# A hybrid decoder layer on one core: conditioning in pieces by contraction rows, u and its first use by token parts

## The chip, the cores and the metric

The kernel runs on one core of a Trainium2 chip. The metric is device time in microseconds. TensorE (PE) multiplies, VectorE (DVE), ScalarE (ACT) and GpSimd (POOL) do the elementwise work, and SyncE (SP) issues most of the DMAs. Data comes from HBM into SBUF (128 partitions); TensorE writes into eight banks of PSUM.

## The reference, cut to what matters

One layer is computed for a prompt of 1024 tokens and for 8 samples of one token each, with the same weights. Both have conditioning vectors c (one for the prompt, eight for the samples), so `mod` has nine rows of 6144.

```python
x = layernorm(x, ln_in_g, ln_in_b)
mod = silu(c) @ w_ada + b_ada                     # 9 x 6144
sh1, sc1, g1, sh2, sc2, g2 = split(mod, 6)
u = x * (1 + sc1) + sh1
proj = u @ w_in          # s_b, s_c, s_h, z, xbc, dt, gates
...                      # short convolution, SSD scan, merged by gates
x = layernorm(ALPHA * x + (1 + g1) * (merged @ w_o), ln_mix_g, ln_mix_b)
u2 = x * (1 + sc2) + sh2
x = layernorm(ALPHA * x + (1 + g2) * moe(u2), ln_ffn_g, ln_ffn_b)
```

Only the first third of `mod` (sh1 and sc1, 2048 columns) is needed to make u; g1 and sh2 (the second third) and sc2 and g2 (the last) are used after the scan. w_ada has 1024 contraction rows and 6144 columns, 25 MB in float32.

## The kernel before

Each engine has one program, written out by hand; the engines wait for each other on semaphores. 1032 tokens (1024 and 8) stand as nine tiles of 128, the last with 8 rows. Contraction over 1024 goes in eight steps of 128 rows (`k`).

**Start.** SP loads c, the x tiles (`load_x`, four buffers) and w_ada in 12 groups of 512 columns, 2 MB each, into three buffers (`load_wada`). DVE's `norm(i)` makes the input layernorm of a tile: statistics, the root on ACT (`std`), then two wide operations (L1223, L1226) with mean, ln_in_g, reciprocal root and ln_in_b. POOL stores the normed tile to `x0_dram` for the residual. On TensorE `mod_group(q)` (L1858) makes 512 columns of `mod` with c as the stationary operand, 9 columns wide, so all results lie in PSUM partitions 0 to 8. DVE adds the bias (`add_mod`, L1231). After four groups TensorE turns the 16 blocks of shift and scale into columns (L1876) and small weight rows too (L1882, L1889). Then `turn_x(i)` (L1868) turns a tile of x, and ACT makes u from it with `scale` and `bias` per partition (`ut`, L903), between the other eight groups. When all is there, TensorE makes the 32 dt columns of all tiles (L1903), ACT and DVE split u into `u_hi` and `u_lo` (L918, L1290), for projections in three parts of a float.

**Turns.** `turn(g)` makes six units of 128 projection columns (x, x, B, C, z, z of a head group), each in three token parts of 344 columns (`SUB`): 18 steps, counted from 0, in the order `STEPS`, a projection of 24 matmuls each (L1912 to L1914). The weights of a unit are split on ACT (`high`, L923) and POOL (`low`, L760), three slots deep. Turn 0 has projections alone, with the sums of dt*A in between (L2009 to L2012) and the spread of the samples' rows (L2015), and DVE's convolutions of its units at its end. Turns 1 to 8 run the SSD scan of the group before beside the projections.

**w_o stage.** Late in the kernel, for each tile, TensorE makes merged @ w_o (L2128), and DVE multiplies by 1 + g1, adds ALPHA times the stored x (L1599), norms and makes u2 (L1596 to L1620).

## Time and profile before

| | us |
|---|---|
| median of 3 runs (2714.0 to 2715.81) | 2715.81 |
| the profiled execution, its own time | 2713.93 |
| its span, first to last instruction | 2711.8 |
| TensorE busy | 2438.1 |
| DVE busy | 1616.0 |
| ACT busy | 1174.5 |
| POOL busy | 544.0 |
| mean granted TensorE clock, share of full | 0.956 |

The busy time of an engine tells little by itself; a stage is read by who waits for whom in it. The time that the whole takes beside the span (2.1 us) lies around the first and the last instruction. Times in the rows below are from the start of the span.

### The profile page before, as it was taken

The numbers are of one execution on the slowest core, as the hardware profiler recorded it, in microseconds if no ns is written. First come the engines' busy times: TensorE is split into PE (matmuls) and PEld (weight loads), VectorE is DVE, ScalarE is ACT, GpSimd is POOL, SyncE is SP. The second block draws the span as 40 slices with busy tenths as digits, with TensorE's granted clock in tenths as the row PEclk, the third lists the DMA queues.
The fourth block names the chain that finished last, engine by engine and source line by source line (L and its number), as shares of the span: only waits on it lengthen the run. The fifth ranks groups of instructions, "written<-read, shape, count | busy, mean of one in ns | idle before, by whom it ended". The sixth has DMA issues, their size and how long they took to land. (4 is left out here: it accounts for less than half of the span.)

```text
span 2711.8 us, 32410 instructions
## 1 busy us (share of the span) xinstructions
PE 2438.1 (90%) x13028; PEld 1994.9 (74%) x13028; DVE 1616.0 (60%) x2502; ACT 1174.5 (43%) x1480; POOL 544.0 (20%) x309
## 2 busy tenths in 40 slices
PE   6889999999999999999999999999579999999960
PEld 2289888888889889666999988855257777777740
DVE  3336988988988983000133321145758888888869
ACT  0334677667677675000000000000147777777751
POOL 0011221221121120000344411100013223232320
PEclk8979999999999999999999999999789999999985
DMA  7722233233233224212111131121369999999963
GB/s 262 271 67 80 62 96 101 59 95 97 63 90 103 63 82 152 67 39 54 39 47 47 47 102 41 30 89 58 121 213 348 340 350 353 354 347 337 339 218 141
DMA packets 255525, 397.56 MB, mean 147 GB/s; under 512 B 17571, under 2 KB 167723, under 8 KB 255321
## 3 DMA queue, kind: packets, MB, share of 16 engines
q1 hardware_dynamic: 232368, 344.63, 38.6%
q0 software_dynamic: 14080, 34.61, 3.3%
q10 hardware_dynamic: 8928, 16.26, 1.9%
q8 instruction: 103, 1.69, 0.3%
q14 instruction: 46, 0.38, 0.0%
HBM read 364.66 MB, written 48.22 MB: 152 GB/s over the span
## 5 line engine op out<-in xcount | busy, mean ns | idle before, releaser
L1912 PE MATMUL bank<-u_hi,w_pairs 128*128 128x344 f32 x1344 | 446.6, 332 | 9.1 <-DVE u_lo L1290 9.1
L1913 PE MATMUL bank<-u_lo,w_pairs 128*128 128x344 f32 x1344 | 431.2, 321 | 0.0
L1914 PE MATMUL bank<-u_hi,w_pairs 128*128 128x344 f32 x1344 | 431.1, 321 | 0.0
L1651 DVE TENSOR_TENSOR we_parts<-u_whole,we_parts 128x2048 fp32r<-128x2048 f32 x129 | 295.1, 2287 | 60.0 <-ACT we_parts L1131 59.7
L1131 ACT ACTIVATE we_parts<-u_whole 128x2048 fp32r<-128x2048 f32 x129 | 247.1, 1917 | 51.5 <-PE bank L2176 26.3
L1912 PEld LDWEIGHTS bank<-u_hi,w_pairs 128*128 128x128 f32 x1344 | 255.2, 190 | 14.0 <-DVE u_lo L1290 9.3
L760 POOL TENSOR_TENSOR w_pairs<-arena,w_pairs 128x1024 fp32r<-128x1024 f32 x56 | 150.7, 2692 | 545.1 <-ACT w_pairs L923 544.9
L1913 PEld LDWEIGHTS bank<-u_lo,w_pairs 128*128 128x128 f32 x1344 | 254.7, 190 | 3.9 <-issue 3.8
L1914 PEld LDWEIGHTS bank<-u_hi,w_pairs 128*128 128x128 f32 x1344 | 254.5, 189 | 0.0
L2034 PE MATMUL bank<-arena 128*128 128x344 f32 x768 | 222.2, 452 | 0.0
L2174 PE MATMUL bank<-we_parts,x_parts 128*128 128x512 f32 x512 | 209.8, 410 | 3.3 <-DVE we_parts L1651 1.9
L2034 PEld LDWEIGHTS bank<-arena 128*128 128x128 f32 x768 | 145.9, 190 | 76.0
L2176 PE MATMUL bank<-we_parts,x_parts 128*128 128x512 f32 x512 | 201.2, 393 | 0.0
L2175 PE MATMUL bank<-we_parts,x_parts 128*128 128x512 f32 x512 | 200.4, 391 | 0.0
L1374 DVE SCALAR_TENSOR_TENSOR arena<-arena 128x512 f32<-128x512 f32 (+3 forms) x192 | 158.9, 827 | 3.4
L1912 PE MATMUL bank<-u_hi,w_even 128*128 128x344 f32 x480 | 155.8, 325 | 2.3 <-DVE arena L1562 1.7
L1651 DVE TENSOR_TENSOR we_parts<-arena,we_parts 128x2048 fp32r<-128x2048 f32 x64 | 146.6, 2291 | 12.0 <-ACT we_parts L1131 12.0
L1913 PE MATMUL bank<-u_lo,w_even 128*128 128x344 f32 x480 | 153.3, 319 | 0.0
L1914 PE MATMUL bank<-u_hi,w_even 128*128 128x344 f32 x480 | 153.3, 319 | 0.0
L1535 DVE TENSOR_TENSOR arena<-arena,bank 128x344 f32<-128x344 f32 x24 | 12.3, 513 | 229.7 <-PE bank L2034 229.7
L1081 ACT ACTIVATE arena<-bank 128x344 f32<-128x344 f32 x24 | 11.0, 458 | 293.2 <-PE bank L1914 293.2
L1003 ACT ACTIVATE arena<-bank 128x344 f32<-128x344 f32 x168 | 74.5, 448 | 138.2 <-PE bank L1914 136.8
(340 smaller groups left out, 5029.5 us busy)
## 6 DMA issues: line engine op xcount, KB each, us to landing
u_whole<-in_w_moe_dram SPq DMA_DIRECT2D x128, 1024.0 KB, 7.4
arena<-in_w_moe_dram SPq DMA_DIRECT2D x64, 1024.0 KB, 7.5
arena<-in_w_in_dram SPq DMA_DIRECT2D x88, 512.0 KB, 5.4
arena<-in_w_ada_dram SPq DMA_DIRECT2D x12, 2048.0 KB, 11.6
arena<-cum_dram ACTq DMA_DIRECT2D x62, 256.0 KB, 3.1
yb_dram<-arena POOLq DMA_DIRECT2D x8, 1032.0 KB, 5.0
arena<-in_state_ssm_dram SPq DMA_DIRECT2D x16, 512.0 KB, 5.6
out_dram<-arena SPq DMA_DIRECT2D x16, 512.0 KB, 4.5
```

What stands on the lines that cost most here:

```text
L760: pool.tensor_tensor(pair_lo[u % 3], wslot[u], pair_hi[u % 3].bitcast(F32), ALU.subtract).then_inc(unit_split, 1)
L1003: act.activation(dst[:, part * SUB:(part + 1) * SUB], banks[s % 3][:, 0:SUB], ACT.Copy).then_inc(raw_ready, 1)
L1131: act.activation(w_his[parts_of(n, j)], wraw[slot], ACT.Copy).then_inc(whi_ready, 1)
L1374: last = dve.scalar_tensor_tensor(dst[:, start:hi], src[:, start - back:hi - back], w(3 - back), dst[:, start:hi], ALU.mult, ALU.add)
L1651: dve.tensor_tensor(w_los[v], wraw[slot], w_his[v].bitcast(F32), ALU.subtract).then_inc(wlo_ready, 1)
L1912: pe.matmul(out, hi[:, k, :], u_hi[:, k, at], start=(k == 0), stop=False)
L1913: pe.matmul(out, hi[:, k, :], u_lo[:, k, at], start=False, stop=False)
L1914: last = pe.matmul(out, lo[:, k, :], u_hi[:, k, at], start=False, stop=(k == KD - 1))
L2034: last = pe.matmul(banks[first + part][:, 0:SUB], wslot[slot][:, k, :], yb[1 - half][:, k, part * SUB:(part + 1) * SUB], start=(half == 0 ...
L2174: pe.matmul(out, xt_hi[b][:, at], w_his[v][:, cols], start=(kk == 0), stop=False)
L2175: pe.matmul(out, xt_hi[b][:, at], w_los[v][:, cols], start=False, stop=False)
L2176: last = pe.matmul(out, xt_lo[b][:, at], w_his[v][:, cols], start=False, stop=(kk == KD - 1))
```

## The change

**Conditioning.** w_ada is loaded in 24 pieces by contraction rows: 128 rows and one third of the columns (2048), 1 MB, with 8 KB in a row. `mod_piece(q)` makes four matmuls of 512 columns per piece; each writes its own 32 partitions of one PSUM bank (`acc[32 * j:32 * j + 32]`), and the stationary c is padded with zeros to 32 columns. A third has eight pieces. The first third is made at the start, the others within the second half of turn 0, one or two pieces behind a projection. The bias is broadcast to 32 partitions four times per third, and DVE adds it in one operation per third. SP stores the last two thirds to `mod_dram` (POOL did it once before).

**u.** ln_in_g and ln_in_b are turned into columns and put into scale and shift; `norm(i)` has one wide operation. Nine x buffers instead of four. ACT (`u_left`) and DVE (`u_right`) make half a tile of u each; `u_high`, `u_low` and `dt_rows` go tile by tile. `x0_dram` then holds x without ln_in_g and ln_in_b; they are applied on DVE in the w_o stage (`residual`), with two more loads of broadcast rows.

**Turn 0.** The first nine steps go by token parts (`STEPS0`); a part starts when the three tiles of u that it needs are split. Tiles 5 to 8 are turned between the first four steps, and dt of tiles 3 to 8 between the first five. ACT makes dt's exponentials behind its ninth copy. DVE adds the second third's bias ahead of the convolutions and the last third's behind them.

```diff
-            r0 = Room(Y0, W0)
-            wada = [r0.take(KD * 512).rearrange("p (k c) -> p k c", k=KD) for _ in range(3)]
-            xr = [r0.take(D) for _ in range(4)]
...
+        xr = [arena[:, XR0 + i * D:XR0 + (i + 1) * D] for i in range(TILES + 1)]
+        wada = [arena[:, 2 * D * x:2 * D * (x + 1)] for x in range(7)] + [arena[:, YST0:YST0 + 2 * D]]
+        late = (YST0, HS0, HS0 + 2 * D)
+        wada += [arena[:, late[x % 3]:late[x % 3] + 2 * D] for x in range(2 * KD)]
...
+        STEPS0 = [(u, part) for part in range(3) for u in range(3)] + STEPS[9:]
...
             def load_wada(q):
-                if q >= 3:
-                    sp.wait_ge(mod_done, q - 2)
-                sp.dma_start(wada[q % 3], w_ada_v[:, :, q * 512:(q + 1) * 512]).then_inc(wada_landed[q % 3], 16)
+                third, k = q // KD, q % KD
+                if q >= 4:
+                    sp.wait_ge(mod_done, q - (2 if q >= 11 else 3))
+                sp.dma_start(wada[q], w_ada_v[:, k, 2 * D * third:2 * D * third + 2 * D]).then_inc(wada_landed[q % 4], 16)
...
+            turn(0, False, range(3))
+            sp.wait_ge(dt_raw, 9)
+            sp.wait_ge(x0_stored, 9 * 16)
+            for third in range(1, 3):
+                load_bada(third)
+            for q in range(8, 11):
+                load_wada(q)
+            turn(0, False, range(3, 6))
+            for q in range(11, 16):
+                load_wada(q)
             sp.wait_ge(cols_copied, 5)
...
+            for q in range(18, 24):
+                load_wada(q)
+            for third in range(1, 3):
+                sp.wait_ge(mod_added, third + 1)
...
-                st.did(dve.scalar_tensor_tensor(x, x, mv[0:rows, i % 4, 0:1], ln_g[0:rows, :], ALU.subtract,
-                                                ALU.mult))
                 st.settle()
-                dve.scalar_tensor_tensor(x, x, mv[0:rows, i % 4, 3:4], ln_b[0:rows, :], ALU.mult,
-                                         ALU.add).then_inc(x0_ready, 1)
+                dve.tensor_scalar(x, x, mv[0:rows, i, 0:1], mv[0:rows, i, 3:4], ALU.subtract,
+                                  ALU.mult).then_inc(x0_ready, 1)
...
+            u_right(0)
+            for i in range(1, TILES + 1):
+                u_right(i)
+                u_low(i - 1)
+            u_low(TILES)
...
+            residual(0)
             for i in range(TILES + 1):
...
                 dve.tensor_tensor(u, u, sh2, ALU.add).then_inc(u2_ready, 1)
+                if i < TILES:
+                    residual(i + 1)
...
+            def mod_piece(q):
+                third, k = q // KD, q % KD
+                pe.wait_ge(wada_landed[q % 4], 16 * (q // 4 + 1))
+                if k == 0 and third:
+                    pe.wait_ge(mod_added, third)
+                acc = banks[(0, 3, 4)[third]]
+                for j in range(4):
+                    last = pe.matmul(acc[32 * j:32 * j + 32, :], c_t[:, k, :], wada[q][:, 512 * j:512 * j + 512],
                                      start=(k == 0), stop=(k == KD - 1))
                 last.then_inc(mod_done, 1)
...
+            for i in range(5, TILES + 1):
+                turn(0, (i - 5,))
+                turn_x(i)
+                if i == 5:
+                    dt_rows(3)
+                dt_rows(i - 1)
+            turn(0, (4,))
+            dt_rows(TILES)
+            turn(0, range(5, 10))
+            mod_piece(8)
+            for s in range(10, 18):
+                turn(0, (s,))
+                if s == 11:
+                    pe.wait_ge(dta_ready, 1)
...
+                if s == 13:
+                    pe.wait_ge(spread_ready, 1)
+                    pe.matmul(bank7, ones[0:NS, :], spread, start=True, stop=True).then_inc(spread_done, 1)
+                    mod_piece(15)
+                else:
+                    q = 2 * s - 11 - (s > 13)
+                    for x in range(2):
+                        mod_piece(q + x)
```

TensorE, the start, before: the c rows are turned (L1848), then groups of the conditioning (`9x512`), small rows (L1876 to L1889), and x turns between further groups.

```order
L1848 MATMUL bank<-arena 128x9 x8
L1858 MATMUL bank<-arena 9x512 x32
L1876 MATMUL bank<-arena 128x9 x16
L1882 MATMUL bank<-arena 128x21 x8
L1889 MATMUL bank<-arena 128x29 x32
L1868 MATMUL bank<-arena 128x128 x8
L1858 MATMUL bank<-arena 9x512 x8
```

And now: L1946 is a matmul of a piece (`32x512`), L1957 a turn of x, L1981 the turn of scale and shift, L1990 dt of a tile. The last two rows come twice more before the first projection.

```order
L1934 MATMUL bank<-arena 128x9 x8
L1946 MATMUL bank<-arena 32x512 x16
L1966 MATMUL bank<-arena 128x23 x8
L1971 MATMUL bank<-arena 128x29 x32
L1957 MATMUL bank<-arena 128x128 x16
L1946 MATMUL bank<-arena 32x512 x16
L1981 MATMUL bank<-arena 128x128 x4
L1957 MATMUL bank<-arena 128x128 x8
L1990 MATMUL bank<-arena,u_whole 128x32 x8
```

Before, all 96 conditioning matmuls and all 72 of dt stood ahead of the first projection; now 32 of the conditioning and 24 of dt do, and the rest is among the projections.

TensorE in turn 0, behind projection 11, in the kernel now: L2004 is the end of that projection, L2113 to L2115 the sums of dt*A, L1946 two pieces, L2002 the next projection.

```order
L2004 MATMUL bank<-u_hi,w_pairs 128x344
L2113 MATMUL bank<-arena 128x128 x2
L2114 MATMUL bank<-arena 128x256
L2115 MATMUL bank<-arena 128x256
L1946 MATMUL bank<-arena 32x512 x8
L2002 MATMUL bank<-u_hi,w_pairs 128x344
```

The sums stood behind projection 5 before, with no pieces around them.

SP's queue of DMAs from the first units' weights to turn 1, before (in brackets the semaphores that an issue waits for):

```order
L497 DMA arena<-in_w_in_dram 128x8x128 [waits mod_added]
L497 DMA arena<-in_w_in_dram 128x8x128 x5
L497 DMA arena<-in_w_in_dram 128x8x128 [waits unit_split] x2
L561 DMA cum_dram<-arena 128x2x128 [waits cols_copied]
L567 DMA arena<-cum_dram 128x512 [waits cum_stored,dt_ready]
L567 DMA arena<-cum_dram 128x512
L520 DMA arena<-in_state_ssm_dram 128x8x128 x2
L497 DMA arena<-in_w_in_dram 128x8x128 [waits unit_split] x4
```

And now:

```order
L487 DMA arena<-in_w_in_dram 128x8x128 [waits unit_split] x3
L483 DMA arena<-in_b_ada_dram 32x512 [waits x0_stored,dt_raw]
L483 DMA arena<-in_b_ada_dram 32x512 x7
L478 DMA arena<-in_w_ada_dram 128x2048 [waits mod_done] x3
L487 DMA arena<-in_w_in_dram 128x8x128 [waits unit_split] x3
L478 DMA arena<-in_w_ada_dram 128x2048 [waits mod_done] x5
L584 DMA cum_dram<-arena 128x2x128 [waits cols_copied]
L478 DMA arena<-in_w_ada_dram 128x2048 [waits mod_done] x2
L591 DMA arena<-cum_dram 128x512 [waits cum_stored,dt_ready]
L591 DMA arena<-cum_dram 128x512
L478 DMA arena<-in_w_ada_dram 128x2048 [waits mod_done] x6
L600 DMA mod_dram<-arena 9x512 [waits mod_added]
```

The 16 loads of w_ada's last two thirds, which stood ahead of the first units, are now spread among turn 0's other issues, each with a wait for a piece made.

## Rows read from the trace of the kernel before

**Rows 1.** The page's busy table: busy us (share of the span), instructions.

```profile
PE 2438.1 (90%) x13028; PEld 1994.9 (74%) x13028; DVE 1616.0 (60%) x2502; ACT 1174.5 (43%) x1480; POOL 544.0 (20%) x309
```

**Rows 2.** Busy time by stage: window, length, PE, PEld, DVE, ACT, POOL, PEclk, DMA, GB/s.

```profile
63.50:135.10 71.60, 64.75 (x193) 17.65 (x193) 27.15 (x55) 24.09 (x70) 3.19 (x6) 0.99 0.76 270
135.10:162.00 26.90, 26.80 (x144) 26.59 (x144) 0.19 (x1) 9.25 (x6) 4.68 (x2) 0.53 0.61 164
...
171.04:243.23 72.19, 72.19 (x443) 71.10 (x444) 33.09 (x57) 23.09 (x38) 14.51 (x6) 0.98 0.21 53
```

**Rows 3.** Order of time, 108 to 117 us: start, us, engine, line, count.

```profile
108.68 1.09 PE L1868 MATMUL bank<-arena 128*128 128x128 f32 x8
...
109.87 2.90 ACT L903 ACTIVATE u_whole<-bank,arena 128x128 f32<-128x128 f32 x8 [3.47 <-PE bank L1868]
...
109.92 7.04 PE L1858 MATMUL bank<-arena 128*9 128x512 f32 x16 [0.15 <-DMA arena<-in_w_ada_dram]
```

**Rows 4.** Order of time, the split of u and the first projection.

```profile
162.03 8.96 DVE L1290 TENSOR_TENSOR u_lo<-u_whole,u_hi 128x2064 fp32r<-128x2064 f32 x4 [26.74 <-PE bank L1903]
...
171.04 0.66 PE L1912 MATMUL bank<-u_hi,w_pairs 128*128 128x344 f32 x1 [9.12 <-DVE u_lo L1290]
```

**Rows 5.** Busy time by stage while the first loads run; DMA share and GB/s last.

```profile
4.00:12.00 8.00, 0.00 (x0) 0.00 (x0) 1.66 (x4) 1.73 (x3) 0.00 (x0) 1.00 1.03 398
12.00:20.00 8.00, 7.75 (x13) 1.44 (x14) 0.00 (x0) 0.00 (x0) 0.00 (x0) 1.00 1.06 195
...
24.00:48.00 24.00, 18.34 (x38) 3.68 (x39) 13.87 (x20) 0.59 (x2) 1.87 (x3) 0.79 1.04 396
```

**Rows 6.** Order of time on DVE: a norm of tile 5, and wide tensor_scalars later.

```profile
77.15 1.29 DVE L1216 BATCH_NORM_STATS2 arena<-arena 128x6 f32<-128x512 f32 x2 [4.65 <-DMA arena<-in_x_prompt_dram]
...
79.12 1.27 DVE L1223 SCALAR_TENSOR_TENSOR arena<-arena 128x1024 f32<-128x1024 f32 x1
...
1779.32 2.51 DVE L1586 TENSOR_SCALAR u_whole<-u_whole 128x1024 f32<-128x1024 f32 x4 [0.21 <-DMA arena<-in_b_route_e_dram]
```

**Rows 7.** Busy time by stage: two x turns, dt, and the first projection's start.

```profile
61.61:63.50 1.89, 1.89 (x9) 1.56 (x8) 0.83 (x4) 0.00 (x0) 0.00 (x0) 0.50 0.01 4
...
116.89:117.90 1.01, 1.01 (x9) 0.85 (x8) 0.68 (x1) 0.00 (x0) 0.00 (x0) 1.00 1.06 389
...
171.04:174.47 3.43, 3.43 (x12) 3.43 (x13) 1.09 (x5) 2.98 (x5) 0.00 (x0) 0.50 0.00 0
...
137.00:162.00 25.00, 24.93 (x129) 24.69 (x128) 0.00 (x0) 7.35 (x6) 4.68 (x2) 0.50 0.57 154
```

**Rows 8.** Order of time on PE in turn 1: matmuls that write 64 partitions each.

```profile
252.27 0.66 PE L1955 MATMUL bank<-arena 128*64 128x128 f32 x8
252.86 0.33 PE L1943 MATMUL bank<-arena 128*128 128x128 f32 x1
```

**Rows 9.** Order of time: the first and the last step of the dt chain.

```profile
171.44 0.45 ACT L932 ACTIVATE arena<-arena 128x288 f32<-128x288 f32 x1 [27.09 <-DVE arena L1296]
...
182.23 0.17 DVE L1329 TENSOR_TENSOR arena<-arena 8x32 f32<-8x32 f32 x1
```

**Rows 10.** Order of time: DVE's first operation of turn 1, in brackets its wait.

```profile
243.97 0.29 DVE L1386 TENSOR_TENSOR arena<-bank,arena 128x128 f32<-128x128 f32 x1 [9.77 <-PE bank L1946]
```

**Rows 11.** DMA issues: 1 MB loads from the page; landing of the w_ada loads.

```profile
u_whole<-in_w_moe_dram SPq DMA_DIRECT2D x128, 1024.0 KB, 7.4
...
DMA to landing us min/median/max: 8.6/11.6/21.2
```

**Rows 12.** The w_o stage: DVE's waits (us, times, longest), a wide operation, the last tile.

```profile
DVE arena L1596 <- PE bank L2128: 63.2, 9, 11.4
...
L1618 DVE TENSOR_TENSOR arena<-arena,u_whole 128x1024 f32<-128x1024 f32 (+1 forms) x9 | 11.0, 1223 | 0.3
...
1919.79 1.28 DVE L1596 TENSOR_TENSOR arena<-bank,u_whole 8x512 f32<-8x512 f32 x2 [7.10 <-PE bank L2128]
```

More of the change, by code:

```diff
@@ L1051, in _ @@
             act.activation(decay, cend, ACT.Exp).then_inc(wend_ready, 1)
-            turn(0, range(7, 18))
+            turn(0, range(12, 18))
             for g in range(1, GROUPS + 1):
@@ L1244, in _, with add_mod @@
+            def add_mod(third):
+                dve.wait_ge(mod_done, KD * third + KD)
+                if third:
+                    dve.wait_ge(small_landed, (16 + 8) * 16)
+                dve.tensor_tensor(mod[third], banks[(0, 3, 4)[third]][:, :], bada[third], ALU.add).then_inc(mod_added, 1)
+            for i in range(4):
+                norm(i)
+            dve.wait_ge(cols_turned, 1)
+            src = bank6[:, 0:KD * (ROWS_C + 2)].rearrange("p (k r) -> p k r", k=KD)
             for a, b in ((0, 3), (19, 21)):
@@ L1282, in _ @@
-            last.then_inc(ut_s_ready, 1)
+            for i in range(4, TILES + 1):
+                norm(i)
+            add_mod(0)
+            dve.wait_ge(cols_turned, 4)
+            dve.wait_ge(cols_copied, 3)
+            turned = banks[5][:, :].rearrange("p (c j m) -> p j c m", c=4, j=4)
+            by_col = dict(j=2)
+            scale4, shift4 = (x.rearrange("p (j c) m -> p j c m", j=2) for x in (scale_t, shift_t))
+            for j in range(2):
+                st.did(dve.tensor_scalar(scale4[:, j], turned[:, 2 + j, :, 0:MROWS], 1.0, None, ALU.add))
@@ L1895, in _ @@
-            turn_x(TILES)
-            pe.wait_ge(ut_ready, TILES)
-            pe.wait_ge(ut_s_ready, 1)
-            for i in range(TILES + 1):
-                rows = P if i < TILES else NS
-                for k in range(KD):
-                    last = pe.matmul(bank7[0:rows, i * HEADS:(i + 1) * HEADS], uT[:, k, i * P:i * P + rows],
-                                     w_dt[:, k, :], start=(k == 0), stop=(k == KD - 1))
-            last.then_inc(dt_raw, 1)
-            pe.wait_ge(u_lo_ready, KD // 2)
+            turn_x(0)
@@ new lines, in _, with dt_rows @@
+            pe.wait_ge(cols_copied, 1)
+            turn_x(1)
+            for q in range(4, 8):
+                mod_piece(q)
+            pe.wait_ge(mod_added, 1)
+            for cb in range(4):
+                last = pe.transpose(banks[5][:, cb * P:(cb + 1) * P], mod[0][:, cb * P:(cb + 1) * P], ident)
+            last.then_inc(cols_turned, 1)
+            def dt_rows(i):
+                rows = P if i < TILES else NS
+                pe.wait_ge(ut_ready, min(i + 1, TILES))
+                pe.wait_ge(ut_s_ready, i + 1)
+                for k in range(KD):
+                    last = pe.matmul(banks[5][0:rows, i * HEADS:(i + 1) * HEADS], uT[:, k, i * P:i * P + rows],
+                                     w_dt[:, k, :], start=(k == 0), stop=(k == KD - 1))
+                last.then_inc(dt_raw, 1)
@@ L1908, in projection @@
+            for i in range(2, 5):
+                turn_x(i)
+                dt_rows(i - 2)
             def projection(out, hi, lo, part):
@@ L1922, in sub @@
                 def sub(s):
-                    u, part = STEPS[s]
+                    u, part = step_of(g, s)
+                    if g == 0 and s in (0, 3, 6):
+                        pe.wait_ge(u_lo_ready, s + 3)
                     if part == 0:
```

337 lines of the change are left out of this document (177 added, 160 removed).

## The prediction

> **What bounds the kernel now.** I read the page's busy table first, then the busy time of each engine by stage, then the order of time at the start. TensorE is busy 90% of the span [rows 1], so the reader looks for the stretches where it works at something that need not be there, or sparsely. The stage table [rows 2] shows one: the first projection of turn 0 starts at 171.04 us. Until then TensorE makes the conditioning, turns x and makes the dt columns. Turn 0 itself then takes 72.19 us with TensorE never idle. So what counts is when turn 1 can begin: 243.23 us now. After it the two kernels run the same projections in the same order, up to the w_o stage, so a gain up to there reaches the end unless that stage gives it back.
>
> Three things lie ahead of 171 us. The conditioning: 12 groups of 16 matmul records, 7.04 us each at the full clock [rows 3], 84 us of TensorE altogether. The dt columns: 26.80 us [rows 2], nearly all at half the clock. And the split of u, which waits for all of them: DVE's 8.96 us with TensorE idle for 9.12 us [rows 4]. The loads are not idle either: 24 to 48 us moved 396 GB/s at a DMA share of 1.04 [rows 5], so the first 40-odd us are near what the DMAs give.
>
> **The change part by part.** I rebuild the time at which turn 1 starts.
>
> *To the scale and shift of u (before: at 55 us, but with the matmuls of the other two thirds following until 133).* Only the first third, 8 pieces of 1 MB, is needed. With x (4.2 MB), the pieces (8.4 MB) and some 0.9 MB of small rows, 13.5 MB must land. At 396 to 398 GB/s [rows 5] that is 34 us from the first issue at 1.5 us; the stretch from 12 to 20 us, where the small rows moved at only 195 GB/s, costs another 4 to 6: the last piece lands near 42. DVE is later than that. It now norms x tiles 4 to 8 before it adds the bias. A norm takes 1.97 us until the first of its two wide operations, which takes 1.27 [rows 6]; now one two-scalar operation stands there for both, which I put at 0.7 to 1.1 us, since a 1024-wide tensor_scalar is at 0.63 (four in 2.51, [rows 6]). So 2.8 us a norm. The five start when the small columns are turned. That stands behind piece 3 (some 26 us) and, at half the clock, 6 to 7 us of turns, so at 33; they end at 47. Bias 0.7, four turns 1.2, six small DVE operations 1.7: **51 us** (45 if the small rows hold up less, 58 if they hold up more). The dropped ln_g and ln_b rows save 1 MB of loads and one wide operation a tile; that is in these numbers.
>
> *Three token tiles before the first projection (before: all nine).* The first projection of a part of 344 columns needs u tiles 0 to 2. TensorE turns x (8 turns: 1.89 us at half the clock, 1.09 at full [rows 3, 7]) and makes that tile's dt (16 records; 129 records took 25 us at half the clock [rows 7], so 3.1 to 3.4). ACT and DVE make half a tile each: ACT's eight took 2.90 [rows 3], so four 1.45. The split of a tile is 1.05 on ACT and 1.2 on DVE and follows tile by tile. TensorE is the slowest: 3 x 5.4 at half the clock, plus 1.5 before and 1.2 behind, is **19 us**; at the full clock 3 x 2.85 + 2.7, so 11.5. I take the half clock, because in the two stretches with such work, 61.61 to 63.50 and 137 to 162, the granted clock was 0.50 [rows 7]. The first projection then starts at 70 us.
>
> *Turn 0 itself:* the same 18 projections in another order, **72 us**, with its first 3.43 us at half the clock [rows 7], as now.
>
> *Moved into turn 0:* turns of four tiles (3 x 1.09 + 0.7) and dt of six (5 x 1.8 + 0.9 at the full clock, twice that at half): **14 us**, up to 28 where the clock falls between projections.
>
> *Sixteen pieces in turn 0.* A piece is 4 matmuls of 512 columns, 8 records. One after another a record takes 0.427 us (7.04/16 with its gap, [rows 3]), so a piece 3.42. Each of the four writes its own 32 PSUM partitions. The nearest row is the one where matmuls write 64 partitions each in turn: 8 records of 128 columns took 0.59 us until the next matmul started [rows 8], while 8 turns of 128 columns on the whole array took 1.01 until the next, from 116.89 to 117.90 [rows 7]. Records of the first start in pairs: four pairs of 0.107 are 0.43, and the rest, 0.16, is the way in and out. So groups run side by side. For four groups I take 2 x 0.427 plus 0.14, **1.0 us a piece, 16 us**. The ends are 0.87 (nothing for the way in) and 1.72 (only two of four side by side).
>
> The Trainium skill, page "TensorE: Matmul & The Clock Gate", section "Measured speedup vs the span model", has 2.38 times for three column tiles, not 3. By that a piece would be an estimated 1.08 us and the term 17 instead of 16. Its row shows less overlap than ours of two groups; no row here shows three or four.
>
> *Loads of these pieces.* They go through three places, a load being issued once the piece three before is made. The 15 pieces from step 10 on have a cover of 8 x 3.8 + 15 x 1.0 = 45 us; with a landing time L they take at least 5 x (L + 1.0). A 1 MB load of this size landed in a median of 7.4 us under a full load of DMAs [rows 11], which gives 42. It just fits; I put **3 us** for single waits (0 to 10).
>
> *Waits added in turn 0.* ACT makes dt's exponentials only behind its copy of projection 8. The chain takes 10.8 us (171.44 to 182.23, [rows 9]), so it is done 12.5 us after projection 8; TensorE asks for it behind three projections and three pieces, 14 us later: hidden by these 1.7 us. Queued behind it on ACT are copies 9 to 11, which TensorE needs three projections on. DVE's bias add of the second third stands ahead of all convolutions; after it DVE has 20 us of them, against 4 projections and 8 pieces, 23 us. They end together with turn 0, where DVE now waits 9.77 us [rows 10]: that cover is nearly used up, and if it is gone turn 1 starts a microsecond or two late. On SP, loads of state, the sums and the third's stores are behind waits for pieces; the state is asked for 30 us into turn 1. Nothing else waits there.
>
> *Two more DVE operations a tile in the w_o stage* (ln_g and ln_b put onto the stored x): 9 x 2 x 1.22 us [rows 12], 22 us of DVE. DVE waits for TensorE 63.2 us over the nine tiles there, 7.1 before the last [rows 12], and TensorE doesn't wait for it. 2.45 fits into each wait: **0**, and 22 if that cover were gone.
>
> *Sum:* 51 + 19 + 72 + 14 + 16 + 3 = **175 us** for the start of turn 1, against 243.2: 68 us less. The profiled execution took 2713.9 us (span 2711.8); 68 off is 2646. The median of the runs shown is 1.9 higher, so **2647 us**.
>
> **The rivals.** (1) *The four column groups run one after another*, so the change doesn't do what its form asks. Then 16 x 2.4 = 39 us come back in turn 0, and some 8 in the start, where pieces 4 to 7 stand behind the turns: 2694. For it speaks that no row has four groups or streams this long; against it the pairs. (2) *Turn 0 is paced by loads.* The 2 MB conditioning loads landed in a median of 11.6 us [rows 11]. With that as L, 5 x 12.6 = 63 against 45: 18 us back, 2665. For it: they go out behind other waits on one queue. Against: half the size, long rows. (3) *The start runs at the full clock*: 7.5 us less there and 1.7 less in the first projection, 2638. (4) *Slower than before*: the same mechanism as (2) with loads that land late enough. It decides from L = 22 us on, since 5 x 23 - 45 is 70, and 2716 or more comes out. The latest load of the conditioning took 21.2 us [rows 11], but it was twice as large and stood behind the small rows.
>
> **How the numbers follow.** Forecast 0.66, (1) 0.09, (2) 0.12, (3) 0.10, (4) 0.02, and 0.01 for a time within 0.2% of before. 0.2% is 5.4 us, about what a measurement of this kernel tells from no change. The likeliest stays: 2647. For the range, the lows (45, 11.5, pieces at 0.87, no waits) would give 2623 if all came together, the highs (58, moved work at half the clock, pieces at 1.72, 10 us of waits) 2686. Not all meet: I take 2628 to 2676. That holds the forecast, (2) and (3) and leaves out (1) and (4). Faster: 0.66 + 0.09 + 0.12 + 0.10 = 0.97; same 0.01; slower 0.02.
>
> **What would show it.** In the changed kernel's rows: the first u_hi projection near 70 us and the first scores of turn 1 near 175; the scale written near 51; the granted clock between 50 and 70 us (0.50 here, 1.00 for (3)); a piece's 8 records starting in fours within about a microsecond, not 0.43 apart; TensorE idle before a piece for its load not above 1 us (more is (2)); DVE still idle before its w_o additions. I am wrong most easily in the start, where the DMAs, DVE's five norms and the clock each can move it by 5 to 8 us.

## The result and the profile after

| | before | changed kernel | forecast |
|---|---|---|---|
| median of four runs, us | 2715.81 | 2648.2 | 2647 |
| lowest and highest run | 2714.0, 2715.93 | 2646.19, 2651.25 | range 2628 to 2676 |
| profiled execution, its own time | 2713.93 | 2651.25 | |
| its span | 2711.8 | 2649.5 | |
| first projection of turn 0 starts (in the span) | 171.04 | 74.78 | 70 |
| first scores of turn 1 start | 243.23 | 180.27 | 175 |

The ratio of the changed kernel to the one before is 0.9754, with a 95% interval of 0.9742 to 0.9766: 67 us less. The profiled execution is the slowest of the four runs. In it turn 1 begins 63.0 us earlier, and the span is 62.3 us shorter, so 0.7 us were given back behind turn 0. The engines' busy line, answering to [rows 1]:

```profile
PE 2383.2 (90%) x13016; PEld 1987.3 (75%) x13016; DVE 1628.0 (61%) x2532; ACT 1164.9 (44%) x1453; POOL 543.3 (21%) x309
```

TensorE is busy 55 us less in all. Busy time by stage (window, length, PE, PEld, DVE, ACT, POOL, PEclk, DMA, GB/s), answering to [rows 2, 5]: the start at half the clock; turn 0 as a whole, then its part with the moved work and its part with the pieces.

```profile
47.80:78.52 30.72, 22.00 (x97) 19.77 (x98) 17.11 (x36) 15.41 (x29) 9.88 (x5) 0.50 0.61 187
74.78:180.27 105.49, 105.16 (x699) 89.70 (x699) 43.95 (x84) 32.99 (x57) 14.15 (x6) 0.95 0.54 193
74.78:111.56 36.78, 36.78 (x249) 36.21 (x249) 11.78 (x24) 11.30 (x22) 2.18 (x1) 0.86 0.06 18
111.56:180.27 68.71, 68.38 (x454) 53.48 (x451) 32.17 (x60) 21.69 (x35) 11.97 (x5) 1.00 0.80 287
```

What was 72 us of turn 0 is 105.49 us now, and TensorE idles for 0.33 us of it, though 287 GB/s of loads run beside its second part.

The order of time on TensorE (start, us, line, count, in brackets the idle time before and who ended it), first from the start, then single pieces and pairs in turn 0:

```profile
30.04 1.93 PE L1946 MATMUL bank<-arena 128*32 128x512 f32 x8 [1.81 <-DMA arena<-in_w_ada_dram]
31.90 1.04 PE L1966 MATMUL bank<-arena 23*128 23x23 f32 x8
...
49.39 1.93 PE L1946 MATMUL bank<-arena 128*32 128x512 f32 x8 [4.36 <-DMA arena<-in_w_ada_dram]
52.14 1.11 PE L1981 MATMUL bank<-arena 128*128 128x128 f32 x4 [0.81 <-DVE arena L1276]
58.17 1.94 PE L1957 MATMUL bank<-arena 128*128 128x128 f32 x8 [4.92 <-ACT u_whole L937]
59.91 3.46 PE L1990 MATMUL bank<-arena,u_whole 128*128 128x32 f32 x16
63.18 1.95 PE L1957 MATMUL bank<-arena 128*128 128x128 f32 x8
...
74.78 0.65 PE L2002 MATMUL bank<-u_hi,w_pairs 128*128 128x344 f32 x1 [1.39 <-DVE u_lo L1353]
...
130.62 1.07 PE L1946 MATMUL bank<-arena 128*32 128x512 f32 x8
...
142.74 1.92 PE L1946 MATMUL bank<-arena 128*32 128x512 f32 x16
```

A piece takes about a microsecond and a pair 1.92, where a group of the conditioning took 7.04 before [rows 3]; a piece holds half as much, so at the full clock 24 pieces at about 1 us stand against 12 groups at 7.04. In the start, at half the clock, a piece took 1.93 us (30.04 and 49.39). In the trace the records of the pair at 142.74 start in fours: 143.197, 143.204, 143.210 and 143.217, and then 143.626, 143.633, 143.639 and 143.646. Each four is 0.43 us behind the last.

The start is late where the forecast was most in doubt. On DVE, POOL and SP:

```profile
8.42 10.49 SPq L483 DMA_DIRECT2D arena<-in_b_ada_dram  x4
18.96 0.50 SPq L478 DMA_DIRECT2D arena<-in_w_ada_dram  x1
...
37.27 1.29 DVE L1263 BATCH_NORM_STATS2 arena<-arena 128x6 f32<-128x512 f32 x2
...
51.39 0.69 DVE L1276 TENSOR_TENSOR arena<-bank,arena 128x512 f32<-128x512 f32 x1
53.29 0.30 DVE L1320 TENSOR_SCALAR arena<-bank 128x36 f32<-128x36 f32 x2 [1.21 <-PE bank L1981]
53.62 0.23 DVE L1322 TENSOR_TENSOR arena<-arena 128x72 f32<-128x72 f32 x1
53.89 0.29 DVE L1325 TENSOR_TENSOR arena<-arena,bank 128x36 f32<-128x36 f32 x2
54.22 2.31 DVE L1327 TENSOR_TENSOR arena<-arena 128x72 f32<-128x72 f32 x1
...
54.10 2.34 POOL L794 TENSOR_TENSOR w_pairs<-arena,w_pairs 128x1024 fp32r<-128x1024 f32 x1 [1.90 <-ACT w_pairs L954]
```

The norms of tiles 4 to 8 run from 37.27 to 51.37, without a gap but for the roots. The last multiply of the scale, L1327, takes 2.31 us, where its equal L1322 took 0.23: it ends with POOL's first split of a weight, which began 0.12 us before it.

### The profile page after: what moved, and what is told of

It reads as the page before. It is cut to its first block and busy times, and to the rows that moved or that the text cites. A ratio compares the mean times of both kernels' runs of the same rounds, so it can differ in the third digit from the quotient of the medians.

```text
span 2649.5 us, 32426 instructions
## 1 busy us (share of the span) xinstructions
PE 2383.2 (90%) x13016; PEld 1987.3 (75%) x13016; DVE 1628.0 (61%) x2532; ACT 1164.9 (44%) x1453; POOL 543.3 (21%) x309
## 5 line engine op out<-in xcount | busy, mean ns | idle before, releaser
L2002 PE MATMUL bank<-u_hi,w_pairs 128*128 128x344 f32 x1344 | 450.4, 335 | 1.4 <-DVE u_lo L1353 1.4
L2004 PE MATMUL bank<-u_hi,w_pairs 128*128 128x344 f32 x1344 | 434.6, 323 | 0.0
L2002 PEld LDWEIGHTS bank<-u_hi,w_pairs 128*128 128x128 f32 x1344 | 257.7, 192 | 12.2 <-issue 10.5
L2004 PEld LDWEIGHTS bank<-u_hi,w_pairs 128*128 128x128 f32 x1344 | 257.1, 191 | 0.0
L2002 PE MATMUL bank<-u_hi,w_even 128*128 128x344 f32 x480 | 155.8, 325 | 2.3 <-DVE arena L1636 1.7
L2004 PE MATMUL bank<-u_hi,w_even 128*128 128x344 f32 x480 | 153.3, 319 | 0.0
```

What stands on the lines that cost most here:

```text
L2002: pe.matmul(out, hi[:, k, :], u_hi[:, k, at], start=(k == 0), stop=False)
L2004: last = pe.matmul(out, lo[:, k, :], u_hi[:, k, at], start=False, stop=(k == KD - 1))
```

## The experiments

All but e10 start from the changed kernel. e1 to e9 have one time each, so effects of a few microseconds are read from their traces: when the first projection and the first scores start, and what lies between.

| | time | first projection | first scores | between |
|---|---|---|---|---|
| changed kernel, profiled | 2651.25 | 74.78 | 180.27 | 105.49 |
| e1, fewer column groups | 2672.24 | 74.42 | 200.69 | 126.27 |
| e2, two late pieces only | 2633.97 | 73.44 | 162.03 | 88.59 |
| e3, whole u first | 2656.65 | 96.35 | 186.02 | 89.67 |
| e4, split behind the scale | 2645.31 | 71.06 | 174.13 | 103.07 |
| e5, all pieces ahead | 2667.51 | 109.71 | 196.06 | 86.35 |
| e6, dense start | 2640.78 | 68.32 | 172.03 | 103.71 |
| e7, stores later | 2643.8 | 69.45 | 174.73 | 105.28 |
| e8, residual left out | 2648.06 | 72.67 | 176.03 | 103.36 |
| e9, start reordered | 2629.65 | 54.98 | 161.29 | 106.31 |
| e10, start and tail | 2630.08 (5 runs) | 56.44 | 160.90 | 104.46 |

From the first scores to the end of the span all of them take 2467 to 2470 us. With nothing changed ahead of them, first projections still differ by 2 us (72.67 to 74.78 in e1, e2, e8 and the changed kernel), and the stretch between by 2 (105.49 against 103.36 in e8). The start of the changed kernel's profiled execution is the latest of these: its last piece starts at 49.39, in e2, e3, e4 and e8 at 46.7 to 46.9 (49.17 in e1). In it the granted clock also fell to 0.50 twice for 3.4 us in the first part of turn 0 (part of the 0.86 above); so it did in e7, once in e8, and not in e4. So 2 or 3 us between two of these times mean little unless a row shows them.

**e1: do the column groups run side by side?**

```diff
-                    last = pe.matmul(acc[32 * j:32 * j + 32, :], c_t[:, k, :], wada[q][:, 512 * j:512 * j + 512],
-                                     start=(k == 0), stop=(k == KD - 1))
+                    n = (4, 1, 2)[third]
+                    r = j if k == 0 else j % n
+                    last = pe.matmul(acc[32 * r:32 * r + 32, :], c_t[:, k, :], wada[q][:, 512 * j:512 * j + 512],
+                                     start=(k == 0), stop=(j >= n if k == 0 else k == KD - 1 and j >= 4 - n))
```

> From the changed kernel: in the second third, every piece but its first sends all four matmuls to column group 0; in the last third to groups 0 and 1 (so g1, sh2, sc2 and g2 are not what they should be). Same matmuls, same loads. Theory (the four groups run side by side, and that is what makes a piece 0.94 us): seven pieces of 3.4 us (8 records one after another at 0.427) and seven of 1.7 to 1.8, so 7 x 2.5 + 7 x 0.8 = 23 us more, 2671 us, first scores of turn 1 at 203 instead of 180.3. Rival A (a piece is short because it is only 32 columns wide, or because of how its rows lie; groups don't matter): pieces stay at 0.9 to 1.0, 2648. Rival B (turn 0 is paced by DVE's convolutions or by loads, TensorE has slack): pieces get longer but the first scores move by less than 15 us.

Two pairs of pieces in its order of time, the first with one column group, the second with two:

```profile
144.89 7.05 PE L1948 MATMUL bank<-arena 128*32 128x512 f32 x16
...
182.05 3.63 PE L1948 MATMUL bank<-arena 128*32 128x512 f32 x16
```

7.05, 3.63 and 1.92 us for the same pair with one, two and four groups: 3.5, 1.8 and 0.96 a piece. From start to next start the pieces hold TensorE 38.9 us in turn 0, against 15.5 in the changed kernel: 23.4 more, 23 expected. The theory holds, rival A falls. Rival B falls too: in this stretch nothing hid the longer pieces. (The stretch as a whole grew by 20.8 against the profiled execution, and by 23.2 against e4, which like e1 had no fall of the clock there.)

**e2: what do the late pieces cost?**

```diff
-            for q in range(8, 11):
+            for q in (8, 16):
                 load_wada(q)
...
+                if q >= 8 and k:
+                    return
```

> From the changed kernel: of the 16 pieces in turn 0 only the first of each third is loaded and made (14 pieces and 14 MB of loads left out; g1, sh2, sc2 and g2 are sums over 128 rows only). Theory (each piece costs its TensorE time, loads cost nothing): 14 x 0.94 = 13 us earlier first scores, 167; DVE's convolutions start behind the spread, some 5.6 us earlier, and end at about 171, so TensorE waits for them for some microseconds early in turn 1: 9 to 13 us in all, 2635 to 2639. Rival A (turn 0 is paced by the convolutions already): only the 3 us that DVE waits now before its last bias add, 2645. Rival B (loads pace it, or contend with turn 0's other work): more than 13 us, 2630 or less.

Between first projection and first scores there are 14.5 us less than in e4, 16.9 less than in the profiled execution; 2634 us. The theory's 13 was short by 1.5 to 4, and its first scores at 167 by 5 (162.03, of which 1.3 is an earlier start); the time lies a microsecond below its 2635 to 2639 and above rival B's 2630. Rival A is out: DVE did end its convolutions after turn 0 then, with the last bias add at 167.39, but TensorE's waits for DVE in the first 48 us of turn 1 were 2.7 us, against 1.8 without the edit. Rival B stays possible for a microsecond or two: taking away 14 MB of loads as well gave slightly more than 14 x 0.94.

**e3: what is the order by token parts worth?**

```diff
-            return STEPS[s] if g else STEPS0[s]
+            return STEPS[s]
...
-            for i in range(2, 5):
+            for i in range(2, TILES + 1):
                 turn_x(i)
                 dt_rows(i - 2)
+            for i in range(TILES - 1, TILES + 1):
+                dt_rows(i)
```

> From the changed kernel: turn 0 in the order of the kernel before (by units), and all nine tiles of u turned, made, split and their dt made ahead of the first projection; conditioning in pieces as in the changed kernel. Theory (TensorE paces the start at 5.0 us a tile at half the clock): five more tiles at 5.0 and the samples' 1.3 to 2.6 ahead of the first projection, which starts near 102 instead of 74.8; the same work is gone from turn 0, where it took about 15 us: first scores near 193, 2660 us. Rival A (the work is only moved, the order by token parts gains nothing): 2648. Rival B (dense turns and dt bring the clock to full after a while): tiles at 2.9, first projection near 91, 2650.

The stretch from the first of the seven turns to the first projection:

```profile
56.65:96.35 39.70, 39.13 (x201) 38.80 (x201) 19.12 (x41) 20.07 (x39) 6.45 (x2) 0.50 0.25 69
```

TensorE is busy all the time and the clock stays at 0.50, so rival B falls. The first projection came at 96.35, not 102: only three whole turns, the samples' turn and six dt steps were added, 24 us, and I had counted five whole tiles. Turn 0 is 13.4 us shorter than in e4. Net 8 us slower than the changed kernel's median. Rival A falls: the same work costs 12 to 16 us inside turn 0 and some 24 ahead of it, since there it runs at half the clock.

**e4: POOL's first split behind the scale.**

```diff
+            pool.wait_ge(cols_copied, 4)
             for m in range(8):
                 low(m // 6, m % 6)
```

> From the changed kernel: POOL's first split of a weight (54.10 to 56.44 us in the changed kernel) waits until scale and shift are written. Theory (DVE's 72-element multiply L1327, 2.31 us where its equal L1322 took 0.23, stood still while POOL worked on SBUF): L1327 takes 0.25, the scale is there at 54.5 instead of 56.5, the first projection starts 2.0 us earlier, 2646. Rival (the operation is slow by itself, or waits for what was before it on DVE): it stays at 2.3 and nothing moves.

```profile
51.98 0.23 DVE L1323 TENSOR_TENSOR arena<-arena 128x72 f32<-128x72 f32 x1
52.25 0.29 DVE L1326 TENSOR_TENSOR arena<-arena,bank 128x36 f32<-128x36 f32 x2
52.58 0.23 DVE L1328 TENSOR_TENSOR arena<-arena 128x72 f32<-128x72 f32 x1
...
52.90 2.35 POOL L794 TENSOR_TENSOR w_pairs<-arena,w_pairs 128x1024 fp32r<-128x1024 f32 x1 [2.22 <-DVE arena L1328]
```

The multiply takes 0.23 us instead of 2.31; the rival falls. In e2, e3, e6 and e8, where POOL's split began 0.5 to 1.3 us ahead of it, it was the equal multiply before it that took long, 1.17 to 1.89 us, and the last one took 0.23. The first scores are 6.1 us earlier, but only 2.1 of that is this edit: the bias add already started 1.6 us earlier, ahead of anything that was edited, and the rest is the clock in turn 0. The Trainium skill, page "SBUF — State Buffer", section "Who interferes with whom", says that a DVE instruction with two SBUF inputs contends with a GpSimd instruction that reads SBUF, and calls the port pair that they share an exclusive lock. The rows agree: both multiplies read SBUF twice, and the one that began beside POOL's split ended with it.

**e5: all pieces ahead of turn 0.**

```diff
+            for q in range(8, 24):
+                load_wada(q)
...
                 turn_x(i)
                 dt_rows(i - 2)
+                for q in range(3 * i + 2, 24 if i == 4 else 3 * i + 5):
+                    mod_piece(q)
+            pe.wait_ge(mod_added, 3)
```

> From the changed kernel: all 24 pieces ahead of turn 0, in column groups as they are; the loads of the last two thirds follow those of the first and of three units' weights at once, their two bias adds stand ahead of the first projection, and the split of u waits for the last piece (its buffers overlap). Nothing else is moved. Theory (deferring buys only what the loads can't hide): 36 MB must move before the last piece at about 400 GB/s, so it lands near 95 us; the first projection starts near 99, turn 0 is 15 to 18 us shorter than 105.5, first scores near 187: 2655 us, so that most of the 68 us gained comes from pieces that are quick and from the order of u, not from deferring them. Rival A (deferring is the main gain, loads and splits pile up ahead of turn 0): first scores at 205 or later, 2673 or more. Rival B (nothing gained by deferring, TensorE has the same work): 2648.

```profile
58.00:99.38 41.38, 30.25 (x186) 10.05 (x185) 2.91 (x9) 3.38 (x10) 0.00 (x0) 0.79 1.03 410
99.38:109.71 10.33, 0.00 (x0) 0.00 (x1) 8.17 (x5) 7.68 (x8) 7.70 (x3) 0.50 0.57 157
```

The windows above are from the second tile on and from the last piece to the first projection. In order of time on DVE and POOL:

```profile
101.48 6.98 DVE L1350 TENSOR_TENSOR u_lo<-u_whole,u_hi 128x1024 fp32r<-128x1024 f32 x3 [25.66 <-ACT u_hi L943]
...
104.37 6.30 POOL L791 TENSOR_TENSOR w_pairs<-arena,w_pairs 128x1024 fp32r<-128x1024 f32 x2 [1.42 <-ACT w_pairs L951]
```

The loads pace it as expected (410 GB/s, DMA share 1.03), but 4 us later than I put it, and then TensorE stands still for 10.33 us where I had 4: three splits of u, 1.23 us each elsewhere, take 6.98 us on DVE because POOL splits weights at the same time. So deferring is worth 16 us here by the first scores of the profiled execution (19 by the median time), between my 7 and rival A's 25; some 6 of the 16 belong to the pile of splits, which comes from the buffers' overlap and not from the loads. Even so the first scores are 47 of the 63 us earlier than before, without deferring anything.

**e6: TensorE kept busy in the start.**

```diff
+            def dense(n):
+                pe.wait_ge(cols_copied, 3)
+                for _ in range(n):
+                    pe.matmul(banks[1][:, :], ident, xr[0][:, 0:512], start=True, stop=True)
...
                 mod_piece(q)
+                dense((0, 1, 5, 2)[q - 4])
...
+            dense(6)
```

> From the changed kernel: 14 more matmuls of 128 x 512 whose result nobody reads, where TensorE waits in the start: 1 behind piece 5, 5 behind piece 6, 2 behind piece 7, 6 behind the turns of scale and shift (0.85 us each at the full clock, made to fit the waits). Theory (the granted clock of 0.50 from 47.8 to 78.6 us follows from TensorE's idleness there): the clock stays full, a tile of u takes 2.85 instead of 5.0 us, and the first projection starts 6.5 us earlier, at 68, itself 1.7 us shorter; 2640 us. Rival A (ACT, with 1.5 + 1.1 us a tile and the splits of weights, paces the tiles then): first projection near 70, 2642. Rival B (the clock follows from something else): 0.50 as before, the matmuls only delay: 2650.

```profile
47.80:57.30 9.50, 9.09 (x30) 3.57 (x29) 8.18 (x21) 3.70 (x9) 3.43 (x3) 1.00 1.11 354
57.30:68.32 11.02, 8.13 (x73) 7.93 (x71) 7.93 (x13) 10.55 (x20) 2.55 (x2) 0.97 0.46 132
```

These are the stretches from where the clock fell before to the turn of x tile 2, and on to the first projection. Tiles in order of time:

```profile
57.30 1.04 PE L1957 MATMUL bank<-arena 128*128 128x128 f32 x8
58.18 1.87 PE L1997 MATMUL bank<-arena,u_whole 128*128 128x32 f32 x16
59.88 1.07 PE L1957 MATMUL bank<-arena 128*128 128x128 f32 x8
```

The clock stays at 1.00 and a tile takes 2.6 to 2.9 us instead of 5.0: rival B falls. First projection at 68.32, as the theory has it. But 1.6 of these 6.5 us lie ahead of the tiles: the scale was there at 54.9 instead of 56.5. Of these 0.5 are the four turns at the full clock, the rest is an earlier bias add and a shorter collision with POOL's split. From the scale to the first projection it took 13.4 us instead of 18.2 (18.2 in e8 too), so the clock gave 5.3 of the 6.5. The tiles alone would have given more: TensorE then waited 2.74 us for the third split of u, which took 2.58 us beside POOL's second split. And the clock fell again, to 0.50 from 67.6 to 74.4 us, so the 1.7 us of the first projection did not come.

**e7: POOL's stores of x behind its first splits.**

```diff
-            for i in range(TILES + 1):
-                pool.wait_ge(x0_ready, i + 1)
-                rows = P if i < TILES else NS
-                pool.dma_start(tile_rows(x0_dram, i), xr[i][0:rows, :]).then_inc(x0_stored, 16)
...
+            pool.wait_ge(cols_copied, 4)
             for m in range(8):
+                if m == 3:
+                    for i in range(TILES + 1):
+                        pool.wait_ge(x0_ready, i + 1)
...
                 low(m // 6, m % 6)
```

> From the changed kernel: POOL stores the normed x tiles (4.2 MB) behind the first three splits of weights instead of ahead of them, and makes the first split behind the scale. Theory (the loads of the first third share the DMAs with these stores): the piece that came last is made at about 42 instead of 49.4, piece 3 some 3 us earlier, so the row turns and DVE's norms 4 to 8 behind them too; with the 2 us of the split behind the scale the first projection starts 5 to 7 us earlier, 2642. Rival A (DVE's five norms set the time whatever lands): only the 2 us, 2646. Rival B (the stores collide with the loads of turn 0 instead): TensorE waits there for pieces, 2648 or more.

```profile
42.69 1.93 PE L1948 MATMUL bank<-arena 128*32 128x512 f32 x8 [3.59 <-DMA arena<-in_w_ada_dram]
48.89 1.12 PE L1983 MATMUL bank<-arena 128*128 128x128 f32 x4 [4.26 <-DVE arena L1278]
```

The last piece starts at 42.69 instead of 49.39 and piece 3 at 26.89 instead of 30.04, both earlier than in any run with the stores in place (46.7 and 28.5 at the least), so the stores had shared the DMAs with the loads. Part of it went by SP's queue: the first bias load held it for 4.0 us here and for 9.0 in the changed kernel (8.1 to 8.4 in e2, e3, e4, e6 and e8), so piece 2's load was issued at 14.07 instead of 18.96. Now TensorE waits 4.26 us for DVE, whose norms end at 48.2: rival A is the next bound behind the theory. In the changed kernel's profiled execution both bounds met at 51.3. The first projection comes 5.3 us earlier than there, but only 1.6 earlier than in e4, which has the same edit of the split. By the start of the bias add (48.16, against 49.77 to 51.39 in the runs with the stores in place) the stores alone are worth 1.6 to 3.2 us, at the lower end of the theory's 3 to 5 or below it, and rival A sets the limit.

**e8: the two operations a tile in the w_o stage left out.**

```diff
-                st.did(dve.tensor_tensor(x0, x0, lng_r[0:rows, :], ALU.mult))
-                st.settle()
-                st.did(dve.tensor_tensor(x0, x0, lnb_r[0:rows, :], ALU.add))
```

> From the changed kernel: ln_in_g and ln_in_b are not put onto the stored x in the w_o stage (18 operations of 1.22 us on DVE left out; all else stays). Theory (they lie in DVE's waits for TensorE): no change, 2648; DVE's wait for TensorE before its w_o additions grows by the 22 us, from 38.7 to about 60. Rival (DVE paces part of the stage): up to 22 us less, above all if TensorE waits for DVE there now.

DVE's wait for TensorE there, first in the changed kernel, then without the operations:

```profile
DVE arena L1681 <- PE bank L2235: 38.7, 9, 6.1
```

```profile
DVE arena L1678 <- PE bank L2232: 58.7, 9, 7.1
```

2648.06 us, no change, and from the first scores to the end of the span it took 2470.2 us against 2469.2. The 22 us of operations stood in DVE's waits; of the 63.2 us of waits before [rows 12] 38.7 were left. The rival falls.

**e9 and e10: a version from what the others showed.** Stores behind the splits; x tiles and pieces loaded ahead of most small rows; three norms behind u's first three tiles; matmuls that keep the clock. SP's order in e9 (eight small rows where the first mark stands, w_dt and three more at the second):

```diff
+            for i in range(3):
+                load_x(i)
+                load_wada(i)
...
+            for i in range(3, 6):
+                load_x(i)
+                load_wada(i)
+            load_bada(0)
+            load_wada(6)
+            load_wada(7)
...
+            for u in range(3):
+                load_unit(u, group_cols(0)[u])
+                load_x(6 + u)
```

> From the changed kernel, all that e4, e6 and e7 point to, and the order of the start: x tiles and pieces loaded ahead of most small rows; the row turns ahead of piece 3; DVE norms six tiles ahead of the bias add and the last three behind u's first three tiles; POOL's stores of x behind the first three splits; nine matmuls that only keep TensorE busy and one more behind the third tile. Theory (the start is bounded first by 12.5 MB of loads, then by a chain of bias add, turns, scale and three tiles at the full clock): the last piece is made near 38, the scale near 41, and the first projection starts near 53 instead of 74.8; turn 0 as before; first scores near 157, 2625 us. Rival A (loads land as late as in e7, 42.7): first projection near 58, 2630. Rival B (the stores, moved into turn 0, or the norms, moved behind the tiles, now hold turn 0): first projection early but first scores at 165 or later, 2634 or more. Rival C (the clock falls all the same): first projection near 60, 2632.

```profile
39.31 1.06 PE L1974 MATMUL bank<-arena 128*32 128x512 f32 x8 [0.43 <-DMA arena<-in_w_ada_dram]
...
40.44 0.69 DVE L1292 TENSOR_TENSOR arena<-bank,arena 128x512 f32<-128x512 f32 x1 [5.70 <-PE bank L1974]
```

2629.65: DVE now waits for the pieces, the scale is there at 43.1, the first projection at 54.98 (53 expected). Turn 0 is 2 to 3 us longer than expected (106.31): TensorE waits there 2.7 us for late pieces and 0.9 for a split of u. The 0.9 is rival B's, since norms now stand ahead of that split; the late pieces are not, for 2.3 of the 2.7 us is the wait for the very last piece, more than 70 us behind the last of POOL's stores. Its load took 8.7 us to land, where the changed kernel's took 5.1; why is open.

e10 makes piece 3 ahead of the row turns and starts the last third earlier in turn 0. TensorE, from e9:

```diff
-            for q in range(3):
+            for q in range(4):
                 mod_piece(q)
...
-            turn(0, range(5, 10))
-            mod_piece(8)
-            for s in range(10, 18):
+            turn(0, range(5, 8))
+            q = 8
+            for s in range(8, 18):
...
+                for x in range((1, 2, 2, 1, 2, 1, 2, 2, 2, 1)[s - 8]):
+                    mod_piece(q)
+                    q += 1
```

> From the kernel of e9: piece 3 made ahead of the row turns (the load of piece 7 waits for it: it was issued at 30.6 us there), DVE's norm 3 ahead of the row copies, one busy matmul less; in turn 0 piece 8 one step earlier, the last third begun behind the spread, only one piece behind the last projection, and the second third's bias added ahead of the spread, so that loads have more time (TensorE waited 3.5 us for them in e9). Theory: piece 7 made near 37 instead of 40.4, first projection near 52 instead of 55, turn 0 some 2 to 3 us shorter, first scores near 155; 2624 us. Rival A (loads land as late whatever is issued when, the DMAs being full): 2629. Rival B (DVE, with two more things ahead of its bias add or the convolutions, holds it): first scores at 159 or later, 2627 or more.

2630.08 over five runs, 0.9689 of before (95% interval 0.9676 to 0.9703), so it beats both kernels; against e9 nothing was gained. Turn 0 did get 1.85 us shorter (the waits for late pieces, 2.7 us in the trace of e9 and not 3.5, fell to 1.1). But the load of piece 3 landed at 24.90, no earlier than in e9 (24.38), and the row turns now stood behind it:

```profile
24.95 1.94 PE L1974 MATMUL bank<-arena 128*32 128x512 f32 x8 [7.02 <-DMA arena<-in_w_ada_dram]
26.81 1.04 PE L1999 MATMUL bank<-arena 23*128 23x23 f32 x8
```

In e9 these turns started at 20.97. The load of piece 7 was issued 3.3 us earlier (26.94 instead of 30.20) and landed no earlier (39.92 and 39.26). Rival A has it: for these loads the issue time did not set when they land. It is no rule, as in e7 loads that were issued earlier did land earlier.

## Why the prediction was right, and where it was not

**Scale and shift: 51 forecast, 56.5 measured.** This is the term that was off. Three things, by their rows. (a) I let 13.5 MB share the DMAs and had the last piece land near 42. I left out POOL's stores of the normed x, 4.2 MB in the same stretch (five of nine tiles, 2.6 MB, had landed by then), and the first weights. It came at 49.4 (46.7 to 49.2 in the other runs with the same start), and e7, with the stores moved, has 42.7. (b) I let the norms of tiles 4 to 8 start at 33 and end at 47. Their length was right (14.1 us for five at 2.8), but they start at 37.27, since the small rows are turned behind piece 3, at 31.90 and not 26, and that piece was issued behind the bias rows that held SP's queue for 10.5 us. In the profiled execution pieces and norms were both late by the same time, in e8 the norms alone were the later (bias add at 50.45, last piece at 46.66), so that mending the pieces alone gives less than it seems (e7). (c) Six small operations, 1.7 us forecast, took 3.2, because one stood 2.1 us beside POOL's split (e4). That the first weight's split would now meet the scale on DVE I had not looked at.

**Three tiles: 19 forecast, 18.3 measured** (56.5 to 74.78), at half the clock as assumed. Rival (3), the full clock, did not come by itself; e6 shows what it is worth: 4.8 us of the 7.5 forecast, the other 2.7 being the wait for the last split, and none of the 1.7 in the first projection.

**Turn 0: 72 + 14 + 16 + 3 = 105 forecast, 105.49 measured.** By starts on TensorE: pieces 15.5 with 0.3 of waiting in it (16 and 3 forecast), moved turns and dt 12.5 (14), projections and sums 77.5 (72). The waits were smaller than I allowed and the projections longer: the clock fell twice behind moved work, for 3.4 us each, and in e4, where it did not fall, projections and sums took 75.4; the 3 us that are left were not taken apart. So the sum was closer than its terms, which is luck.

**Column groups.** The step from two groups in [rows 8] to four was right: 0.94 to 0.96 us a piece against 1.0 forecast (7.04/16 is 0.44 and not 0.427, but records do start 0.43 apart), and e1 measured the ends as well: 1.8 with two side by side, 3.5 with one, against 1.72 and 3.42. Rival (1) is out. The Trainium skill, page "TensorE: Matmul & The Clock Gate", section "Measured speedup vs the span model", has 2.38 for three column tiles; the measured gain here is 1.9 for two and 3.7 for four, nearer to the full number.

**Loads of the late pieces.** Rival (2) and (4) needed landing times of 11.6 and 22 us. The 16 loads landed in a median of 6.5 us (4.8 to 9.1), near the 7.4 of the working, and TensorE waited for one of them, 0.3 us. But the margin was small, as the working said: the last load was there 0.5 us ahead of its use, and in e9, where it took 8.7 us instead of 5.1, the waits were 2.7 us.

**Waits in turn 0.** The dt chain ended at 137 us on DVE, ten behind projection 8, and TensorE asked at 141.3: hidden. DVE's convolutions ended at 177.3, three microseconds ahead of turn 0, and DVE waited 3.15 us there where it had waited 9.77 [rows 10]; "nearly used up" was right, and e2 shows that a few microseconds beyond it would have cost about one.

**The w_o stage: 0 forecast, 0 measured** (e8).

**Where the 67 us came from.** The first projection starts 96.3 us earlier and turn 0 is 33.3 us longer, which gives the 63 us of the profiled executions. TensorE's conditioning fell from 89.9 us busy (84, had all of it run at the full clock) to 29.0, of which 13.2 lie in the start between waits for loads. e1 took back 23 us in turn 0, though only seven of its pieces ran in one group and seven in two. Deferring two thirds is worth 16 to 19 (e5), the order by token parts about 8 (e3). These overlap, and the rest was not taken apart. That the median came so near the forecast is luck in part: the profiled execution, whose sum I forecast at 2646, took 5 us more, just what the start was late, and the median lies 3 below it. One sum of the range does not come out: the lows that it names add up to 18.6 us, which is 2628 and not 2623.

## What to carry to other kernels

When a stage waits for loads, add up every byte that moves in it, stores on other queues included, before saying when the last one lands. A thin stationary operand (here 9 columns) is cheapest in column groups: the same pair of pieces took 7.05, 3.63 and 1.92 us in one, two and four. And moving work from a sparse start into a dense stage pays twice, since here it ran at half the clock ahead of turn 0 and mostly at the full clock inside.

## What the runs showed of the hardware that was not expected

*A DVE operation can stand still for POOL.* A 72-element multiply took 2.31 us beside POOL's split and 0.23 without (e4); a split of u on DVE took 2.58 instead of 1.23 (e6); and POOL's split, 2.34 us alone, took 3.2 where DVE's came first. An operation that takes its data from PSUM was not held: L1336 took 1.36 us beside that split, as it did without (64.61).

```profile
68.48 1.23 DVE L1353 TENSOR_TENSOR u_lo<-u_whole,u_hi 128x1024 fp32r<-128x1024 f32 x1 [2.51 <-PE bank L1990]
68.70 3.22 POOL L794 TENSOR_TENSOR w_pairs<-arena,w_pairs 128x1024 fp32r<-128x1024 f32 x1 [12.26 <-ACT w_pairs L954]
69.63 1.36 DVE L1336 TENSOR_SCALAR u_whole<-bank,arena 128x128 f32<-128x128 f32 x4
```

*The granted clock of the first 41 us is not to be taken from the profile.* It reads 1.00 there, but the records of the pieces say otherwise. Minimum, median and maximum in ns of a piece's records, 7 to 32 us and 129 to 146 us in the changed kernel:

```profile
L1946 PE MATMUL bank<-arena x32: 1033/1061/1062, 7.8 to 30.9; 128*32 128x512 f32 x32
```

```profile
L1946 PE MATMUL bank<-arena x40: 592/592/617, 130.6 to 144.1; 128*32 128x512 f32 x40
```

The same matmuls take 1.79 times as long in the first stretch, as at 49.39, where the clock is shown as 0.50. The trace's first entry of the clock begins at 41.01 us, with 1.00, and the pieces change there: their records take 1062 ns from 39.90, 711 to 721 from 40.76 and 593 from 41.31. So the clock was at the lower level until then, and 1.00 stands where there is no entry.

*SP's queue can stand on an issue.* Four bias loads of 64 KB held it for 10.49 us, 9.0 of it the first one, with some 4 MB issued ahead of them, and a small broadcast row in e10 for 6.25 us. What is queued behind such an issue starts that much later. The bytes ahead do not settle it: in e9 the same four loads, with some 10 MB issued ahead, took 1.82 us. In e7, without POOL's stores, the first one took 4.0. What sets it is open.
